# A two-layer hybrid encoder on one core: cross-attention moved into the query and key units, memory's output gate beside its loop

## What is computed

```python
def hybrid_layer(x, mem, positions, w_in, ...):
    proj = x @ w_in
    (r_q, r_k, r_v, r_z, s_u, s_z, m_x, m_v, m_o, m_z, m_i, m_f, a_q, a_z) = jnp.split(proj, ...)
    ret = retention(r_q, r_k, r_v, positions) * silu(r_z)          # rotary q, k; chunks of 64
    s5o = s5(s_u, ...) * silu(s_z)                                  # complex diagonal scan, gelu, GLU
    xc = silu(causal_conv(m_x, ml_conv_w))
    q, k = xc @ ml_wq, xc @ ml_wk
    h = mlstm(q, k, m_v, m_i + b_ig, log_sigmoid(m_f + b_fg)) * sigmoid(m_o)
    ml = head_norm(h) * ml_gn * silu(m_z)
    mk, mv = jnp.split(mem @ xa_w_kv, 2, axis=-1)                   # 256 memory tokens
    xa = memory_attention(a_q, mk, mv) * silu(a_z)                  # 4 heads of 128
    y = jnp.concatenate([ret, s5o, ml, xa], -1) @ w_out
    return layer_norm(ALPHA * x + y, ln_g, ln_b)
```

## Time and profile before

| | |
|---|---|
| device time, median of 3 runs (lowest, highest) | 2037.26 us (2032.01, 2037.69) |
| the profiled execution's own time, and its span | 2037.46 us, 2035.7 us |
| TensorE busy, weight loads | 1874.8 us (92%), 1631.9 us (80%) |
| VectorE, ScalarE, GpSimd busy | 1053.2 us (52%), 620.7 us (30%), 550.3 us (27%) |
| chain that ended last | TensorE 73%, VectorE 11%, DMA 5%, ScalarE 4%, GpSimd 3% |
| mean granted TensorE clock | 0.969 of 2.4 GHz |

### The profile page before, as it was taken

How to read it: one execution, slowest core, us unless ns; L and a number is a source line. 1 busy time by engine, 2 the same in 40 slices (tenths; PEclk the granted TensorE clock), 3 DMA queues, 4 the chain that set the end, 5 groups by cost and what they waited for, 6 DMA issues and landing times.

```text
span 2035.7 us, 27361 instructions
## 1 busy us (share of the span) xinstructions
PE 1874.8 (92%) x11136; PEld 1631.9 (80%) x11136; DVE 1053.2 (52%) x1998; ACT 620.7 (30%) x874; POOL 550.3 (27%) x250
## 2 busy tenths in 40 slices
PE   4898999999999986889989989999999999878997
PEld 4777898899888875767877778988998798656786
DVE  8957634333643775218747666245136458632334
ACT  3332224320143043433233322423112421533320
POOL 4423203131213021145433322132112312102451
PEclk9998999999999998999999989999999999988999
DMA  7333234231221213384343332531302122136541
GB/s 254 103 104 111 82 104 167 93 105 42 63 73 65 89 49 109 107 294 150 128 147 100 105 98 76 172 135 53 104 22 104 62 78 65 55 109 248 175 145 62
DMA packets 95627, 224.35 MB, mean 110 GB/s; under 512 B 10376, under 2 KB 40408, under 8 KB 94480
## 3 DMA queue, kind: packets, MB, share of 16 engines
q1 hardware_dynamic: 70528, 172.58, 26.8%
q10 hardware_dynamic: 24896, 49.82, 6.8%
q0 software_dynamic: 80, 0.23, 0.0%
HBM read 164.13 MB, written 54.23 MB: 107 GB/s over the span
## 4 chain that ended last, share of the span: by engine, by line
PE 73%; DVE 11%; DMA 5%; ACT 4%; POOL 3%; issue 3%; SPq 0%; ACTq 0%; DVEq 0%
PE gp L541 17%; PE gp L543 17%; PE gp L542 17%; POOL wlo L1029 3%; DMA wraw<-in_w 2%; PE mm L541 2%; PE mm L543 2%; PE mm L542 2%; DMA yraw<-yt 2%; PE mm L821 1%; ACT whi L1121 1%; PE mm L665 1%; PE mm L948 1%; PE mm L648 1%; PE mm L667 1%
## 5 line engine op out<-in xcount | busy, mean ns | idle before, releaser
L1029 POOL TENSOR_TENSOR wlo<-wraw,whi 128x1024 fp32r<-128x1024 f32 x172 | 444.9, 2603 | 1178.1 <-ACT whi L1121 1177.9
L541 PE MATMUL gp<-whi,xh 128*128 128x256 f32 x1280 | 383.7, 300 | 0.0
L542 PE MATMUL gp<-wlo,xh 128*128 128x256 f32 x1280 | 363.5, 284 | 0.0
L543 PE MATMUL gp<-whi,xl 128*128 128x256 f32 x1280 | 363.4, 284 | 0.0
L541 PE MATMUL gp<-xh,whi 128*128 128x512 f32 x768 | 324.6, 423 | 5.5 <-issue 3.4
L543 PE MATMUL gp<-xh,wlo 128*128 128x512 f32 x768 | 304.0, 396 | 0.0
L542 PE MATMUL gp<-xl,whi 128*128 128x512 f32 x768 | 303.8, 396 | 0.0
L541 PEld LDWEIGHTS gp<-whi,xh 128*128 128x128 f32 x1280 | 246.8, 193 | 11.3 <-issue 9.9
L542 PEld LDWEIGHTS gp<-wlo,xh 128*128 128x128 f32 x1280 | 247.0, 193 | 5.9 <-issue 5.7
L543 PEld LDWEIGHTS gp<-whi,xl 128*128 128x128 f32 x1280 | 246.3, 192 | 0.0
L1121 ACT ACTIVATE whi<-wraw 128x1024 fp32r<-128x1024 f32 x172 | 175.3, 1053 | 169.6 <-DMA wraw<-in_w 88.7
(11 more groups left out here) (313 smaller groups left out, 3084.3 us busy)
## 6 DMA issues: line engine op xcount, KB each, us to landing
wraw<-in_w SPq DMA_DIRECT2D x172, 512.0 KB, 3.8
spill<-gate ACTq DMA_DIRECT2D x32, 512.0 KB, 2.6
yraw<-yt SPq DMA_DIRECT2D x32, 512.0 KB, 6.3
gate<-spill SPq DMA_DIRECT2D x16, 512.0 KB, 4.8
xs<-xr SPq DMA_DIRECT2D x16, 512.0 KB, 4.1
xr<-in_x ACTq DMA_DIRECT2D x8, 512.0 KB, 7.0
...
```

The costliest lines, as they stand in the source:

```text
L541: nc.tensor.matmul(out, ah, bh, start=start, stop=False)
L542: nc.tensor.matmul(out, ah, bl, start=False, stop=False)
L543: return nc.tensor.matmul(out, al, bh, start=False, stop=stop)
L1029: nc.gpsimd.tensor_tensor(wlo[slot(l, u)][:, 1024 * i:1024 * i + 1024], wraw[n % 2], whi[slot(l, u)][:, 1024 * i:1024 * i + 1024].bitcast( ...
```

## The change

1. **Order of units.** MK, MK+1, x transposes, SU, MV, MV+1, SU+1, the S5 units SZ, SZ+1, AQ, AQ+1, RZ, then RZ+1, GL, GL+1, QK, QK+1, RV, RV+1, LV, MX, LZ, LO, LO+1, AZ, AZ+1. The attention's queries (AQ) go to DRAM and come back as the tiles aq.
2. **Cross-attention** moves, step for step, from the hooks of AZ and AZ+1 to those of QK and QK+1, with XS[j] = 2 + 8j//5. Its result xo is stored to DRAM and loaded again as xg, where x_gate multiplies it by the gate of AZ.
3. **IF** comes after QK+1; its weights wifr are split after the last eviction of QK+1. The gate rows come after the rotary products on VectorE, and row_columns moves from RV to RV+1.
4. **Memory's output gate** is evicted into gate0 and gate1 without a way through DRAM, as `memorise` now runs in the hooks of LO and LO+1. AZ and AZ+1 keep only ml_rows, at hooks 14, 16, ... 28, with four buffers yml, four PSUM tiles and four ring tiles.
5. **Third slot first.** The first output-projection unit (NUNIT) uses slot 2 and is split and subtracted during AZ; y_load(2) and y_load(3) are issued before raw(NUNIT + 2).
6. **S5 steps**: s_inputs(2q+1) at step 1 of ten (was 3), t_rows at 2 (was 4), t_kernel at 4 (was 5), kd and bc loads and t_store at 7 (was 8).
7. **Layer boundary**: unit MK+1 of the next layer is split one output unit earlier.

```diff
-S5_UNITS = (U_SZ, U_SZ + 1, U_RZ, U_RZ + 1, U_LO)
+S5_UNITS = (U_SZ, U_SZ + 1, U_AQ, U_AQ + 1, U_RZ)
-XS = [7 * j // 4 for j in range(XSTEPS)]
+XS = [2 + 8 * j // 5 for j in range(XSTEPS)]
+MLH = [14 + 2 * k for k in range(8)]
...
         def slot(l, u):
-            return (u + l) % 2 if u < NUNIT else ((0, 1, 2), (1, 0, 2))[l % 2][(u - NUNIT) % 3]
+            return u % 2 if u < NUNIT else (2, 0, 1)[(u - NUNIT) % 3]
```

On SyncE's queue, at AZ:

```diff
-                raw(l, U_AZ + 2)
                 sp.wait_ge(S["m_h"], 2 * NC * l + 2 * NC)
-                ring_load(l, 0)
-                ring_load(l, 1)
-                raw(l, U_AZ + 3)
-                ring_load(l, 2)
-                ring_load(l, 3)
+                for i in range(4):
+                    sp.dma_start(ring[i], dram["spill"][D_LZ + i]).then_inc(S["ring_in"], 16)
+                for h in range(HEADS):
+                    sp.dma_start(xg[h], dram["spill"][D_XO + h]).then_inc(S["xo_in"], 16)
+                raw(l, U_AZ + 2)
                 y_load(0)
                 y_load(1)
-                raw(l, NUNIT + 2)
+                raw(l, U_AZ + 3)
                 y_load(2)
                 y_load(3)
+                raw(l, NUNIT + 2)
```

On TensorE:

```diff
-                unit(l, U_SU)
-                unit(l, U_SU + 1, first_tables)
+                unit(l, U_SU[0])
+                unit(l, U_MV)
+                unit(l, U_MV + 1)
+                unit(l, U_SU[1], first_tables)
...
+                unit(l, U_QK, lambda i: attend(i))
+                unit(l, U_QK + 1, lambda i: attend(16 + i))
                 pe.wait_ge(S["wif_hi"], l + 1)
                 pe.wait_ge(S["wif_lo"], l + 1)
...
-                unit(l, U_AZ, lambda i: attend(i))
-                unit(l, U_AZ + 1, lambda i: attend(16 + i))
+                unit(l, U_AZ, lambda i: ml_rows(i))
+                unit(l, U_AZ + 1, lambda i: ml_rows(16 + i))
```

On ScalarE, in `split`, and at AZ:

```diff
-                        act.wait_ge(S["o_used"], NOUT * (l - 1) + 14 + 2 * u)
+                        act.wait_ge(S["o_used"], NOUT * (l - 1) + 14 + u)
...
+                split(l, U_AZ + 1)
+                lo_evict(U_LO + 1, 1)
+                split(l, NUNIT)
+                act.wait_ge(S["hn_var"], 2 * l + 2)
+                F(sd[:, 0:32], mv.rearrange("p (n k) -> p n k", k=2)[:, :, 1], ACT.Sqrt, bias=misc(M_GNE)).then_inc(S["hn_sd"], 1)
+                z_evict(U_AZ, 0)
+                for i in range(9, 16):
+                    ml_rows(i)
+                z_evict(U_AZ, 1)
+                split(l, NUNIT + 1)
```

On VectorE, at AZ:

```diff
+                dve.wait_ge(S["hn_sd"], 2 * l + 2)
+                V.link(nc.vector.reciprocal(sd[:, 0:32], sd[:, 0:32]))
+                lz_gate(0)
+                lz_gate(1)
+                x_gate(0)
+                lz_gate(2)
+                x_gate(1)
+                lz_gate(3)
+                x_gate(2)
```

More of the change, by code:

```diff
@@ L379, in _ @@
                 bc_load(l, 1)
[L380 to L384 removed]
+                for u in range(U_MV + 1, U_SZ + 2):
+                    raw(l, u)
+                    if u == U_SZ:
+                        sp.wait_ge(g_done[1], NUNIT * l + U_MV + 2)
+                        uu_load(l, 0)
+                        uu_load(l, 1)
                 bc_load(l, 2)
@@ L592, in _ @@
                 pe.wait_ge(S["mem_lo"], l + 1)
-                for u in range(U_MK, U_SU):
-                    unit(l, u)
+                unit(l, U_MK)
+                unit(l, U_MK + 1)
                 if l:
@@ new lines, in x_values @@
+                def x_values(j):
+                    h = j // 4
+                    pe.wait_ge(S["x_pt"], XSTEPS * l + j + 1)
+                    if j == 0:
+                        pe.wait_ge(S["mv_in"], 16 * l + 16)
+                    if j:
+                        pe.wait_ge(S["x_pvev"], XSTEPS * l + j)
+                    for m in range(2):
+                        last = nc.tensor.matmul(bank[3][:, 0:256], mvT[:, GW * m + 128 * h:GW * m + 128 * h + 128],
+                                                pt[j % 2][:, 256 * m:256 * m + 256], start=m == 0, stop=m == 1)
+                    last.then_inc(S["x_pv"], 1)
@@ L1489, in _ @@
                 yhi(1)
-                act.wait_ge(gate_used[1], NGATE * l + 5)
-                evict(l, U_AZ + 1, 1, gate[1], gp[1], ACT.Silu)
-                split(l, NUNIT + 1)
+                z_evict(U_AZ + 1, 1)
+                split(l, NUNIT + 2)
                 yhi(2)
@@ L1495, in _ @@
                 x_store(3)
-                split(l, NUNIT + 2)
                 yhi(4)
```

641 lines of the change are left out of this document (303 added, 338 removed).

## The result

The changed kernel runs in 2014.4 us (median of 4 runs, 2009.65 to 2023.83), the kernel before in 2037.47 (4 runs, 2032.01 to 2040.32): a ratio of 0.9894, 95% interval 0.9873 to 0.9915 (the two medians alone give 0.9887). The profiled execution took 2015.2 us with a span of 2013.3, against 2035.7. The forecast was 2009 in a range of 1995 to 2029.

The account below looks back on a forecast made before the run. TensorE's matmuls were taken to bound the kernel, leaving idle time and lost clock to win; -11.7 - 9.6 - 6.5 - 5.5 - 4.0 + 8.5 + 3.1 - 2.8 = -28.5 us gave 2009 us, range 1995 to 2029.

Parts of the forecast that it names:

- What bounds the kernel: Whole kernel: TensorE busy 1874.8 of 2035.7 us, all matmuls stay, only some 161 us idle and lost clock can be won.
- Attention into QK: QK to AZ+1: moving attention saves 11.7 us in layer 0 and 9.6 in layer 1, after new waits.
- IF: Ahead of IF: gate weights split only after the last attention step, 4.7 us of waiting, 2 more of clock.
- 8% of 111.6, 8.9 us, was lost: Layer 0's old attention units: mean clock 0.92 taken as 8.9 us lost, leaving 35.0 us for attention and mLSTM rows.
- the wait at hook 14: In AZ: TensorE waits 6.5 us (4 to 10) for the first gate, 3 of clock follow.
- SyncE waits for the last memory step: SyncE's queue at AZ's start T: after this step ten loads need 12.9 us, the last landing about T + 17.8.
- Beside GpSimd's wlo: VectorE in AZ: four scalings took 3.25 us and the gate 3.27, so the first gate at T + 30.6 at worst.
- the slower rival: AZ: VectorE's scalings, gates and x_gates all slowed beside GpSimd, +20 us a layer, 2050 us; chance of slower 0.07.
- The drain that the Trainium skill adds to a table load: ScalarE's Sqrt before hook 14: about 1.38 us per load, 2.8 us over both layers, left out of the sum.
- Third slot first: Output projection: first unit ready and y loads ahead remove a 5.06 us wait; -6.5 and -5.5 us.
- S5 steps: S5 units: earlier kd load removes a 3.35 us wait, VectorE has less time; net -2 us a layer.
- Front and boundary: Layer start: +8.5 us in layer 0, +3.1 in layer 1; layer boundary, earlier MK+1 split: -2.8 us.

Follow-up runs that it names:

- e3: Changed kernel with the gate weights' split moved from behind QK+1's last eviction into QK+1; 2004.55 us against 2014.4.
- e1: Changed kernel with the head norm's Sqrt ahead of NUNIT's split on ScalarE instead of behind it; 2016.63 us against 2014.4.
- e12: Changed kernel with the four ring products moved from GpSimd to VectorE, the Sqrt left behind NUNIT's split; 2015.54 us against 2014.4.
- e5: Changed kernel with part 5's slots and part 7's split wait undone, the new order of loads on SyncE's queue kept; 2003.94 us against 2014.4.
- e4: Changed kernel with part 6, the S5 step order, alone undone on all engines; 2028.3 us against 2014.4.
- e7: Changed kernel with MV and MV+1 again ahead of the x transposes and SU at a layer's start; 2009.82 us against 2014.4.

## Why the prediction was right in sum and wrong in a part

1. *What bounds the kernel.* Right in the main: the 11136 matmuls stayed, and what moved was idle time, clock and, by the exchange of LO and AQ, 2.5 us between stages. The 27 us that the text puts behind the last matmul are 10.8 in the trace; no term used them.
2. *Attention into QK.* The steps themselves ran as foreseen: three waits of 0.6, 2.2 and 1.5 us, 4.3 in all, against 4. IF: 4.15 against 4.7, and e3 gave it back with its clock. Two terms failed. Together they are the 8.9 us by which layer 0's -11.7 missed -2.8; that the smaller differences cancel out beside them is chance. The first is the step "8% of 111.6, 8.9 us, was lost": 4.6 was, since the rest of the low clock lay over idle time; 4.3 us of work were missing from the 35.0. The second is the wait at hook 14, 11.1 instead of 6.5, 4.6 us. Of its steps "SyncE waits for the last memory step" had the time T, and it is T + 7, for that step comes late and meets AZ+1's wlo. This makes the 4.6: the Sqrt ended 5.3 us later than foreseen and TensorE came 0.5 later, while what stands behind the Sqrt on VectorE took what I had given it. But "Beside GpSimd's wlo" would have failed next. It took the price of a group of scalings and its gate from the earlier trace rows; beside that gate GpSimd was at this work (timeline of the kernel before):

```profile
787.17 4.63 POOL L1054 TENSOR_TENSOR ring<-ring,gn 128x1024 f32<-128x1024 f32 x2 [6.88 <-DMA ring<-spill]
```

The gate of 3.27 us at 789.61 stood beside a ring product and not beside a wlo, and of the four scalings at 777.89 only the first met GpSimd. The sum had the four ring products, 9.4 us in one piece behind their loads, nowhere (only the slower rival counts them). As e1 and e12 show, with an early Sqrt they hold hook 14 for 9.6 us, and with the products moved the late Sqrt holds it for 10.4, so putting one of the two right brings next to nothing.
3. *The drain that the Trainium skill adds to a table load* (ScalarE: Activation LUTs, section What ACT_TABLE_LOAD costs). In the changed kernel the Sqrt starts at 795.44, 1.29 us after its table load began at 794.15, as before without a pause, so leaving the 1.38 us out was right.
4. *Third slot first.* The size was right (-7.4 and -5.0, boundary included in the first, against -9.3 and -5.5), but of its two causes, the ready first unit and the y loads ahead, the first is not needed: e5 shows the same output projection without the slot. In the sum of the change the slot is a loss, 10 us with what it does to AZ, though e5 gives up part 7's gain beside it.
5. *S5 steps.* Mis-sized, -12.8 against -4.0. I had weighed waits against waits. Idle time fell by 2.1 us in layer 0, as I had it, and by 3.7 in layer 1; TensorE's busy time fell by 4.2 and 2.9 us, for which I had no term. By the estimate above 2.5 of each is the exchange of LO for AQ, which I had not priced; what is left goes with the clock. e4 confirms that the step order matters, by its total and by layer 1.
6. *Front and boundary.* +7.1 against +8.5, each step within 2 us (SU+1 starts at 99.8, foreseen 101.5); e7 gives 4.6 of it back in the median, 6.8 at the place. The boundary's wait fell by 2.8 as said. Layer 1's front, +3.1 forecast, was -0.6. The new wait of 2.8 us at MV+1 is there, but waits of 1.29 us at MV and 0.60 at the transposes went, and TensorE's busy time there fell from 76.5 to 74.9 us, at clock 0.96 instead of 0.94.
7. *Rivals.* The slower one named the mechanism behind the second cause at hook 14, VectorE's scalings under GpSimd, though it is the first group and not all of them. The Trainium skill (SBUF — State Buffer, section SBUF: two separate sides) calls the shared port an exclusive lock for a whole instruction. The trace agrees: a 128x2 operation took 2.39 us, and eight scalings 14.51.
